# Summing the experts' results on the chip instead of scattering them to memory and reading them back

## What is computed

```python
g_val, g_idx = lax.top_k(softmax(hf @ w_router_group), 1)      # 4 groups of 8 experts
e_val, e_idx = lax.top_k(softmax(le_sel), 2)                   # 2 experts of 32 for each token
w_tok = g_val * e_val / sum(e_val)
y_e   = (silu(x @ w_e_gate[e]) * (x @ w_e_up[e])) @ w_e_down[e]     # 1024 -> 512 -> 1024
x     = x + segment_sum(y_rows * row_w, row_tok)               # each token gets its two rows
x     = rmsnorm(x, norm_final_g)
```

## Time and profile before

| | us |
|---|---|
| median of 3 runs | 1799.57 (1795.98 to 1802.80) |
| the profiled execution | 1800.18 |
| its span | 1798.3 |
| PE, DVE, ACT, POOL busy | 1661.2, 747.4, 615.1, 133.9 |
| first silu to last silu of the experts | 648.28 to 1100.76 |
| mean DMA rate from 648 to 1100 | 425 GB/s |

### The profile page before, as it was taken

How to read it: one execution, slowest core, us unless ns; L and a number is a source line. 1 busy time by engine, 2 the same in 40 slices (tenths; PEclk the granted TensorE clock), 3 DMA queues, 4 the chain that set the end, 5 groups by cost and what they waited for, 6 DMA issues and landing times.

```text
span 1798.3 us, 21260 instructions
## 1 busy us (share of the span) xinstructions
PE 1661.2 (92%) x8323; PEld 1215.3 (68%) x8323; DVE 747.4 (42%) x1398; ACT 615.1 (34%) x1073; POOL 133.9 (7%) x199
## 2 busy tenths in 40 slices
PE   6999999999999798898778877899999999999899
PEld 5888888888888643333323333688788888988677
DVE  3544345544564521010101012772646643446782
ACT  4122225444441411111111112655353232457760
POOL 0000001001000001111111110010011000000320
PEclk9999999999999899999999998999999999999999
DMA  7665364653226779999999998233123342322102
GB/s 151 88 102 95 105 94 71 67 65 61 68 106 241 276 300 426 427 426 427 427 427 426 428 425 309 103 98 102 35 70 94 94 142 87 98 70 92 54 2 70
DMA packets 115123, 325.91 MB, mean 181 GB/s; under 512 B 8213, under 2 KB 81685, under 8 KB 102224
## 3 DMA queue, kind: packets, MB, share of 16 engines
q1 hardware_dynamic: 109232, 313.76, 52.3%
q0 software_dynamic: 4784, 8.13, 1.2%
q10 hardware_dynamic: 1008, 2.65, 0.4%
HBM read 317.97 MB, written 14.69 MB: 185 GB/s over the span
## 4 chain that ended last, share of the span: by engine, by line
PE 37%; DMA 14%; ACT 2%; DVE 2%; issue 1%; SPq 0%; ACTq 0%; DVEq 0%; POOL 0%; POOLq 0%
DMA up<-in_w_e_up 13%; PE bank L1424 7%; PE bank L1426 7%; PE bank L1425 7%; PE bank L1732 3%; PE turned L1424 2%; PE turned L1425 2%; PE turned L1426 2%; PE bank L1505 1%; PE bank L1758 1%; PE bank L1870 1%; PE bank L1964 1%; PE bank L1539 1%; PE turned L1505 1%; DMA y_tok<-y_dram 0%
## 5 line engine op out<-in xcount | busy, mean ns | idle before, releaser
L2004 DVE TENSOR_TENSOR w_lo<-w_raw,w_hi 128x2048 fp32r<-128x2048 f32 (+1 forms) x72 | 156.8, 2179 | 288.5 <-ACT w_hi L912 279.1
L912 ACT ACTIVATE w_hi<-w_raw 128x512 fp32r<-128x512 f32 (+3 forms) x138 | 169.6, 1252 | 291.6 <-DMA w_raw<-in_w_in 103.6
L1732 PE MATMUL bank<-gate,xt 128*64 128x512 f32 x512 | 225.4, 593 | 25.0 <-DMA up<-in_w_e_up 25.0
L1733 PE MATMUL bank<-up,xt 128*64 128x512 f32 x512 | 225.9, 594 | 0.0
L2326 DVE TENSOR_TENSOR gated_h<-gu_silu,bank 64x512 f32<-64x512 f32 x32 | 22.1, 690 | 391.3 <-ACT gu_silu L1126 391.3
L1732 PEld LDWEIGHTS bank<-gate,xt 128*64 128x64 f32 x512 | 68.6, 137 | 165.1 <-issue 165.1
L1424 PE MATMUL bank<-h1T_hi,w_hi 128*128 128x512 f32 x376 | 151.0, 402 | 0.0
L1758 PE MATMUL bank<-down,hT 128*64 128x512 f32 x256 | 129.8, 655 | 22.2 <-DVE hT L2333 22.2
L1426 PE MATMUL bank<-h1T_hi,w_lo 128*128 128x512 f32 x376 | 146.9, 391 | 0.0
L1425 PE MATMUL bank<-h1T_lo,w_hi 128*128 128x512 f32 x376 | 146.6, 390 | 0.0
L1759 PE MATMUL bank<-down,hT 128*64 128x512 f32 x256 | 129.8, 655 | 0.0
(11 more groups left out here) (691 smaller groups left out, 3659.2 us busy)
## 6 DMA issues: line engine op xcount, KB each, us to landing
down<-in_w_e_down SPq DMA_DIRECT2D x32, 2048.0 KB, 35.6
up<-in_w_e_up SPq DMA_DIRECT2D x30, 2048.0 KB, 38.0
gate<-in_w_e_gate SPq DMA_DIRECT2D x30, 2048.0 KB, 33.3
w_raw<-in_w_in SPq DMA_DIRECT2D x24, 1024.0 KB, 10.0
w_raw<-in_a_w_in SPq DMA_DIRECT2D x20, 1024.0 KB, 5.4
w_raw<-in_w_in SPq DMA_DIRECT2D x16, 512.0 KB, 10.5
w_raw<-in_a_w_out SPq DMA_DIRECT2D x8, 1024.0 KB, 5.1
w_raw<-in_w_conv_out SPq DMA_DIRECT2D x4, 1024.0 KB, 5.1
```

Of the source, the lines that this page charges most:

```text
L912: return nc.scalar.activation(out, in_, ACT.Copy, scale=scale)
L1732: g_ins = pe.matmul(out[0:CAP, :], x, ring_gate[p][:, c, :], start=c == 0, stop=c == KC - 1)
L1733: u_ins = pe.matmul(out[CAP:, :], x, ring_up[p][:, c, :], start=c == 0, stop=c == KC - 1)
L2004: V.tensor_tensor(ring_view(w_lo, n), ring_view(raw, n), ring_view(w_hi, n).bitcast(F32), ALU.subtract)\
```

## The change

The scatter, `y_dram` and the reload go. A new small table `slot_w` gives each slot of each expert its token's weight (a third set of the 16-column matmuls that made the slot table, on PE behind gate_up(0)). ACT now copies the expert's result out of PSUM times that weight, and the two experts of a pair stand in the two halves of `y_s`. ACT and DVE split `y_s` into a high and a low fp32r part. DVE makes `hot_tok`, a table of 128 slots by 512 tokens with a one where the slot holds the token. PE multiplies the two (`sums`, eight pieces of 128 tokens by 512 values, two fp32r matmuls each) while it works on the next even expert, and DVE adds each piece to the residual rows `x1_tok` (`adds`). The last pair's sums come behind the loop, as fp32 matmuls. The banks are dealt out anew: gate and up have bank 2 alone, down bank 6 alone, and the sums go round five banks. POOL makes the low part of one slice of weights that DVE made before. SP waits for the weight table before it loads `gfin` and expert 3.

```diff
+SUM_BANKS, LAST_BANKS = (4, 5, 7, 0, 3), (4, 5, 7, 0, 3, 1, 2, 6)
+SUMS = 2 * TT
...
+        y_s = at("y_s", [P, D], F32, BASE + 2 * BIG + 8192)
+        y_low = at("y_low", [P, D], F32R, BASE + 2 * BIG + 8192)
+        y_high = at("y_high", [P, D], F32R, BASE + 2 * BIG + 12288)
...
+        gu_bank = lambda e: bank[2]
...
+        y_bank = lambda e: bank[6]
...
             sp.wait_ge(sem("over_made"), 1)
+            sp.wait_ge(sem("slot_w_summed"), 1)
             sp.dma_start(gfin[:, :], t["norm_final_g"].unsqueeze(0).to_broadcast([P, D])).then_inc(gfin_loaded, 16)
             for e in range(DEPTH, NE):
                 load_gate(e)
...
-            for tt in TILES2:
-                sp.dma_start(y1_tok[:, tt, :], y_v[0, :, tt, :]).then_inc(sem(f"y1_loaded{tt}"), 16)
-                sp.dma_start(y2_tok[:, tt, :], y_v[1, :, tt, :]).then_inc(sem(f"y2_loaded{tt}"), 16)
...
-                put_rows_of(e)
-                pool.wait_ge(y_made, e + 1)
-                scatter(e % 2)
...
-            pool.wait_ge(scattered, 16 * (NE + 2))
-
+            pool.wait_ge(sem("last_left_made"), 1)
+            pool.wait_ge(sem("last_right_made"), 1)
...
+            pool.wait_ge(w_hi_made, splits_before(slices1) + 1)
+            nc.gpsimd.tensor_tensor(ring_view(w_lo, slices1), ring_view(raw, slices1), ring_view(w_hi, slices1).bitcast(F32), ALU.subtract)\
+                .then_inc(w_lo_made, 1)
...
             def y_rows(e):
+                q, rows = e // 2, half_rows(e % 2)
                 act.wait_ge(left_done, e + 1)
                 act.wait_ge(right_done, e + 1)
-                act.wait_ge(scattered, 16 * max(e - 1, 0) + 32)
-                copy(ys[e % 2][:, 0:512], y_bank(e)[0:CAP, :])
-                copy(ys[e % 2][:, 512:1024], y_bank(e)[CAP:, :]).then_inc(y_made, 1)
+                if e == 0:
+                    act.wait_ge(sem("slot_w_made"), 1)
+                if e >= 2 and e % 2 == 0:
+                    act.wait_ge(sem("summed"), SUMS * q)
+                copy(y_s[rows, 0:512], y_bank(e)[0:CAP, :], slot_w[0:CAP, e:e + 1]).then_inc(sem("last_left_made") if e == NE - 1 else y_made, 1)
+                if e < NE - 1:
+                    copy(y_s[rows, 512:1024], y_bank(e)[CAP:, :], slot_w[CAP:, e:e + 1]).then_inc(y_made, 1)
+                if e % 2 == 1 and e < NE - 1:
+                    for a in range(2):
+                        act.wait_ge(y_made, 2 * e + a + 1)
+                        copy(y_high[:, 512 * a:512 * a + 512], y_s[:, 512 * a:512 * a + 512]).then_inc(sem("y_high_made"), 1)
...
+                    if q >= 2:
+                        pe.wait_ge(sem("added"), SUMS * (q - 1))
...
+                    if e >= 1:
+                        pe.wait_ge(gated_made, e)
...
+                if e >= 1:
+                    pe.wait_ge(y_made, 2 * e)
...
+            def slot_weights():
+
+                pe.wait_ge(sem("hot_w_made"), 1)
+                for b, slots in enumerate((hot_slot, hot_back)):
+                    for q in range(TOPK * TT):
+                        pe.matmul(turns_of(bank[5][0:CAP, 0:NE], b), slots[:, q, :], turns_of(hot_w[:, q, 0:NE], b),
+                                  start=q == 0, stop=q == TOPK * TT - 1)
+                for q in range(TOPK * TT):
+                    ins = pe.matmul(bank[5][0:CAP, NE:NBLK], hot_slot[:, q, :], hot_w[:, q, NE:], start=q == 0, stop=q == TOPK * TT - 1)
+                ins.then_inc(sem("slot_w_summed"), 1)
+
+            def sums(q, ks):
+
+                for k in ks:
+                    tt, cols_ = tile_half(k)
+                    if k == 0:
+                        pe.wait_ge(sem("hot_tok_made"), q + 1)
+                    if q == NE // 2 - 1:
+                        pe.wait_ge((sem("last_left_made"), sem("last_right_made"))[k % 2], 1)
+                    elif k < 2:
+                        pe.wait_ge(sem("y_low_made"), 2 * q + k + 1)
+                    if q == 0 and k == 0:
+                        pe.wait_ge(sem("slot_w_made"), 1)
+                        pe.wait_ge(drained[7], moe_drained(7))
+                    if q < NE // 2 - 1 and SUMS * q + k >= len(SUM_BANKS):
+                        pe.wait_ge(sem("added"), SUMS * q + k - len(SUM_BANKS) + 1)
+                    who = hot_tok[:, tt * P:(tt + 1) * P]
+                    if q == NE // 2 - 1:
+                        ins = pe.matmul(sum_bank(q, k)[:, :], who.bitcast(F32), y_s[:, cols_], start=True, stop=True)
+                    else:
+                        pe.matmul(sum_bank(q, k)[:, :], who, y_high[:, cols_], start=True, stop=False)
+                        ins = pe.matmul(sum_bank(q, k)[:, :], who, y_low[:, cols_], start=False, stop=True)
+                    ins.then_inc(sem("summed"), 1)
...
+                if e % 2 == 0 and e >= 2:
+                    q = e // 2 - 1
+                    gate_up(e, range(5))
+                    for c in range(5, KC):
+                        sums(q, [c - 5])
+                        gate_up(e, [c])
+                    sums(q, (3, 4, 5))
+                    h_turn(e)
+                    sums(q, (6, 7))
+                else:
+                    gate_up(e, range(KC))
+                    if e == 0:
+                        slot_weights()
+                    elif e + 1 < NE:
+                        x_turn(e // 2 + 1)
+                    h_turn(e)
                 down(e)
...
             pe.wait_ge(moe_done, 1)
 
-            idle_turns(bank[6], 22)
-            for a in range(2):
-                pe.matmul(bank[3 * a][:, :], ident, x1_tok[:, TILE_ON_PE, a * 512:(a + 1) * 512], start=True, stop=False)
...
+            idle_turns(bank[1], 4)
+            sums(NE // 2 - 1, range(SUMS))
+            pe.wait_ge(sem("x2_gained"), TT - 1)
+            idle_turns(bank[4], 24)
...
+            def slot_columns():
+
+                dve.wait_ge(sem("slot_w_summed"), 1)
+                V.tensor_copy(slot_w[0:CAP, :], bank[5][0:CAP, 0:NBLK])
+                V.tensor_copy(slot_w[CAP:, :], bank[5][0:CAP, 0:NBLK]).then_inc(sem("slot_w_made"), 1)
+                for a in range(SEQ // CAP):
+                    ins = V.tensor_scalar(all_tok[:, CAP * a:CAP * a + CAP], iota, float(CAP * a), None, ALU.add)
+                step(ins)
+
+            def token_hot(q):
+
+                if q >= 1:
+                    dve.wait_ge(sem("summed"), SUMS * q)
+                V.tensor_scalar(hot_tok[:, :], all_tok[:, :], slot_tok[:, q:q + 1], None, ALU.is_equal).then_inc(sem("hot_tok_made"), 1)
+
+            def y_lows(q):
+                for a in range(2):
+                    part = slice(512 * a, 512 * a + 512)
+                    dve.wait_ge(sem("y_high_made"), 2 * q + a + 1)
+                    V.tensor_tensor(y_low[:, part], y_s[:, part], y_high[:, part].bitcast(F32), ALU.subtract).then_inc(sem("y_low_made"), 1)
+
+            def adds(q, ks):
+                for k in ks:
+                    tt, cols_ = tile_half(k)
+                    dve.wait_ge(sem("summed"), SUMS * q + k + 1)
+                    V.tensor_tensor(x1_tok[:, tt, cols_], x1_tok[:, tt, cols_], sum_bank(q, k)[:, :], ALU.add).then_inc(sem("added"), 1)
+
             for e in range(NE):
-                gated(e)
-                if e % 2 == 1 and e + 1 < NE:
-                    x_copy(e // 2 + 1)
-                h_copy(e)
+                q = e // 2
+                if e % 2 == 0 and e >= 2:
+                    adds(q - 1, range(3))
+                    gated(e)
+                    adds(q - 1, (3,))
+                    h_copy(e)
+                    adds(q - 1, range(4, SUMS))
+                else:
+                    gated(e)
+                    if e % 2 == 1 and e + 1 < NE:
+                        x_copy(q + 1)
+                    h_copy(e)
+                    if e == 0:
+                        slot_columns()
+                    else:
+                        token_hot(q)
+                        if e < NE - 1:
+                            y_lows(q)
...
+            V.tensor_scalar(y_s[CAP:, 512:1024], y_bank(NE - 1)[CAP:, :], slot_w[CAP:, NE - 1:NE], None, ALU.mult).then_inc(sem("last_right_made"), 1)
...
             dve.wait_ge(moe_done, 1)
-            split(slices1, n_slices)
...
-                step(V.scalar_tensor_tensor(out=x1_tok[:, tt, :], in0=y1_tok[:, tt, :], scalar=tok_w[:, 0, tt:tt + 1],
-                                            in1=x1_tok[:, tt, :], op0=ALU.mult, op1=ALU.add))
...
+            dve.wait_ge(gfin_loaded, 16)
+            for tt in range(TT):
+                adds(NE // 2 - 1, (2 * tt, 2 * tt + 1))
+                dve.wait_ge(sem("added"), SUMS * (NE // 2 - 1) + 2 * tt + 2)
+                V.tensor_tensor(x2g_tok[:, tt, :], x1_tok[:, tt, :], gfin[:, :], ALU.mult).then_inc(sem("x2_gained"), 1)
```

More of the change, by code:

```diff
@@ L293, in build_kernel @@
         tok_w = misc("tok_w", [P, 2, TT], F32)
-        table = misc("table", [CAP, NBLK, 2], I32)
+        table = misc("table", [CAP, NBLK, 1], I32)
         get_row = misc("get_row", [2 * CAP, 1], I32)
```

(32 more changed lines are left out.)

131 lines of the change are left out of this document (36 added, 95 removed).

## The result

The changed kernel takes 1807.83 us (median of 13 runs), the kernel before 1800.82 (13 runs on the same chip): a ratio of 1.0035, with a 95% interval from 1.0025 to 1.0045. It is slower by a third of a per cent, and 19.3 us slower than I forecast. The profiled execution has a span of 1808.1 us against 1798.3. One of the 13 executions of the changed kernel took 4439.3 us, for a reason that the record doesn't show, and the ratio leaves it out.

The account below looks back on a forecast made before the run. The prediction took PE early and DMA later to bound the expert loop, the two limits being close, with a serial tail behind. From 1800.18, loop 2.5 and tail 9.0 off gave 1788.7, median 1788.5 us; range 1780 to 1801.

Parts of the forecast that it names:

- PE's sum of a pair: Expert loop: PE's time for two experts rises from 26.6 to 29.0 us, with the last silu at 1098.3.
- its term for the changes of array shape: Pieces between gate chunks: 0.1 us per change, 0.5 a pair; upper bound 0.16 for 8 changes, 1.3.
- dips of the clock put at nothing: Loop: the change fills the gaps followed by 1.2 GHz; no dips counted, each that stays costs 1.5 us.
- PE's matmuls themselves: Loop: the sums' fp32r matmuls start 0.23 us apart, 16 a pair, 3.7 us.
- Pieces 6 and 7 with DVE's add: Loop: these pieces fill the wait for h_copy and cost 0.4 us; DVE's add of piece 3 costs 0.05.
- Pieces 3 to 5: Loop: their 1.4 us fill PE's 1.40 us wait for silu and gated, so they cost nothing.
- The weight table: Expert 0: 48 passes on PE, 3.3 us, partly hidden in a gap, add 1.9 us.
- DMA's sum: Loop: scatters' removal saves 9.7 us, later loads cost 3.1 and gfin in line 2.4; last silu at 1096.6.
- The tail: Behind the loop, from ACT's start on the last result: var 9.6 us earlier; the tail gives 9.0 in all.
- The rival: Tail: the gains wait for POOL's subtraction, later gains come 1.7 us late, tail gives 7.3, total 1790; chance 0.12.
- PE's limit takes the gain back: Loop: changes cost 0.16 each or some clock dips stay; 29.8 us a pair, total 1800; chance 0.16.
- slower: Loop: inserted matmuls run at 0.43 us each, 3.2 more a pair, total 1836; chance 0.07.

Follow-up runs that it names:

- experiment 1: Changed kernel with sums pieces 0 to 2 in one block behind the fifth gate chunk: pairs 29.03 us, ratio 1.001 (executions 1789.8 to 1793.4 or 1813.1 to 1816.6).
- experiment 3: Changed kernel with idle transposes ahead of and behind h_turn in odd experts 3 to 29: 1802.85 us, ratio 1.0007.
- experiment 7: Kernel before without its 32 scatters, reading rows of x in place of the experts' results: 1789.84 us, ratio 0.9922.
- experiment 2: Changed kernel with the sums and adds of pairs 0 to 14 left out: 1787.61 us, ratio 0.9931.
- experiment 10: Changed kernel with pieces behind the gate chunks, h_copy first, odd gaps filled and early split (1787.89 us), plus gfin's load moved behind expert 31's weights: 1787.58 us.
- the second profile of before: The kernel before profiled once more, unchanged: 1797.26 us, tail 24.39 us against 26.22 in its first profile.
- experiment 4: Changed kernel with the slice's high part made by ACT before the last scaling and POOL's subtraction during the last down: 1805.7 us, ratio 1.0032.

## Why the prediction was wrong, point by point

- **The step that failed is PE's sum of a pair, its term for the changes of array shape (0.5 us).** I took 0.1 each from the one change that a row showed, gate to transposes, and counted five; three visits there and back and the way to pieces 3 to 5 are seven. Measured: 0.35 for each visit there and back, 1.05 for the three pieces between chunks (experiment 1). The row showed only the way in. The low matmul's late start and the slow first gate pass were not in it. Together with the gap's 0.13 and 0.09 more for pieces 6 and 7 the clean pair is 29.75, 0.75 over my 29.0, and 15 pairs make 11.3 us. My upper bound, 0.16 for each of eight, gave the rival's 29.8, nearly the value measured; I had it and gave it 0.16.
- **The second failure is in the same sum: dips of the clock put at nothing.** I argued that the change fills the gaps in which the clock was lost. It does, and the even gaps lost no more; but four odd gaps, undisturbed in the earlier trace rows, lost 1.7 us each (I had priced one at 1.5). 6.8 us in this execution; filling the odd gaps removed them all (experiment 3). 11.3 + 6.8 = 18.1 is the 18.0 by which the 15 pairs missed.
- **PE's matmuls themselves were right**: 0.23 apart, also in the block of experiment 1. Pieces 6 and 7 with DVE's add cost 0.54 against 0.45. Pieces 3 to 5 were hidden but for 0.13. The weight table cost 1.3 and not 1.9: silu 0 to 1 took 14.40 us against 13.13, with a granted clock of 1.00 from 652 to 661 us both times. In seven of the experiments with the table it took 16.1, and in experiment 7, without the table, 14.81; in all of these the clock of that stretch was 0.81. So the lowered clock costs 1.7 there, and the table 1.3 at either level. My sum had no dip there either.
- **DMA's sum** was about right in its end, 1096.6, by two wrong terms that cancelled: luck. From silu 0 to the last silu it takes off 9.7 and adds 5.5, 4.2 less. Experiment 7 takes off 6.4 (at most 8.0), and experiment 2, with DMA at its limit and the late start in it, 4.5; so the late start costs 1.9 to 3.5 by these two and 1.1 by experiment 10, not 5.5. With the sums out, the last silu came at 1098.66, or at 1096.3 less the 2.35 by which that profile's first silu was later than before's (650.63, experiment 2). The gain was there, and PE could not use it: the sentence that the two limits were near was true, and a PE sum wrong by 0.75 a pair was enough to turn the sign. That is what I should have weighted: the loop's result hung on one term taken fifteen times, whose two bounds gave 29.0 and 29.8.
- **The tail** was forecast at 9.6 to var and gave 9.2, by two errors that mostly cancelled, which is luck again; against the second profile of before it gave 7.4. The first sums ran at full clock, so that the first gain was ready 1.7 earlier than I took; then it waited for POOL, 2.7 more. That makes 8.6, and 0.6 is not accounted for. The rival had the mechanism and priced it at 1.7: it had POOL's end nearly right (7.8 us behind ACT's start, measured 7.2), but the gain was ready 4.4 us behind that start and not 6.1, as the sums were faster. The Trainium skill (SBUF — State Buffer, on the shared port pair) says that a VectorE instruction with two inputs in SBUF and a GpSimd one that reads SBUF shut each other out. The rows here agree: the gain takes 3.91 beside POOL's 4.53, and the two adds beside the same instruction, with one input in PSUM, their usual 1.45. With POOL out of the way the gain takes 1.22 (experiment 4), 2.7 less. I had this rival, at 0.12.
- **Of the rivals**, "PE's limit takes the gain back" is what happened, 29.8 a pair and dips that stay. It named both causes with an "or"; both came, and 1800 became 1808. No sums' matmul started 0.43 behind another, so the rival "slower" had the sign by another mechanism.

## What to carry to other kernels

Small matmuls put between large ones of another array shape and number format cost more than their own time: here 0.35 us a visit for 0.46 us of work. Put them in one block, and that block where the engine waits anyway; the same work then went from 1.0035 to 0.9941, some of it by clock not lost. When a change frees one limit and loads another that is within a per cent of it, work out both with the upper bound of each unknown first, and multiply by the trips: fifteen times 0.75 us was more than the whole tail gave. And a gap that is filled can move the loss of clock to the next gap, so look at each of them.

## What the runs showed of the hardware that I had not expected

- The price of a change from 64-column halves in fp32 to the full array in fp32r and back is spread over four starts (0.10, 0.11, 0.09, 0.05 us), so that no one row shows it; it is the same 0.35 for one piece and for three. A third of it (the low matmul's late start) came also with the format alone.
- Of gaps with the same content (0.31 and 0.90 us idle), four of 15 were followed by passes at the lower clock, each worth 1.7 us; an undisturbed pair or more lay between any two of them. In another execution of the same loop it was two of 15. One kernel had twelve executions on two levels, 1792 and 1815 us, and span times mean clock was the same 1766 to 1768 us on both. A fall in nearly every pair of the loop would give it (14 x 1.7 = 24), but where the clock was lost was not shown; which gap falls and which doesn't is open.
- Giving a full queue of loads an earlier start gained 1.1 us and not 5.5: soon after, the loads moved 343 GB/s instead of 429 for 12 us, most likely because they waited for slots that PE frees.
- A VectorE instruction held off by GpSimd is seen as a long instruction (3.91 instead of 1.23 us), not as a wait: none of the views of waits names it.
